# Four small moves in a float32 kernel: Gelu tiles, paired spatial products, late sums of squares, one square on ScalarE

## The reference

```python
# first block, layers 0 and 1
h = rmsnorm(x, g_pre); u, z = split(h @ w_in)            # 2048 -> 2 x 4096
y = pool_mixer(u) if layer 0 else rglru(causal_conv(u))
x = x + rmsnorm((y * silu(z)) @ w_out, g_post)
gate = sigmoid(rmsnorm(x, g_ple_in) @ w_ple_gate)        # 2048 -> 2048
x = x + rmsnorm((p @ w_ple) * gate, g_ple_out)
# second block, layers 2 and 3
proj = rms_norm(x, norm_g) @ w_in
y_a = mla(c_q, c_kv, k_rope) * silu(z_a)                 # attention, 8 heads
y_b = gelu(u_b) * mix(rms_norm(gelu(v_b), v_g)) * silu(z_b)
#     mix: per chunk of 128 tokens and per group of 128 features,
#     tril(w_s) @ v + b_s, 8 groups
y_c = gla(q_c, k_c, v_c, a_r) * silu(z_c)                # gated linear attention, 4 heads
x = x + (sum of sigmoid(gate_b) * (y_b @ w_branch_b)) @ w_out
```

## Time and profile before

| what | us |
|---|---|
| timed runs, median of 3 | 3372.26 (3371.91 to 3381.12) |
| the profiled execution's own time | 3364.99 |
| span of the profiled execution | 3363.2 |
| TensorE matmul busy | 3326.3 (99%) |
| VectorE busy | 2299.5 (68%) |
| ScalarE busy | 1680.0 (50%) |
| GpSimd busy | 947.9 (28%) |

### The profile page before, as it was taken

The page is one execution under the profiler, slowest core; times in us unless marked ns, Lnnn a source line. Parts: engine busy times, 40 slices in busy tenths (PEclk is TensorE's granted clock), DMA queues, the critical chain, the costliest instruction groups (busy, mean ns, idle before and its releaser), DMA issues.

```text
span 3363.2 us, 67501 instructions
## 1 busy us (share of the span) xinstructions
PE 3326.3 (99%) x28712; PEld 3313.3 (99%) x28712; DVE 2299.5 (68%) x3008; ACT 1680.0 (50%) x2122; POOL 947.9 (28%) x901
## 2 busy tenths in 40 slices
PE   8999999999999999999999999999999999999999
PEld 8999999999999999999999999999999999999999
DVE  7876654688888845877867755555568777655554
ACT  5334444555588745655544444444456444444443
POOL 3952320144556500513523200000016222100000
PEclk9999999999999999999999999999999999999999
DMA  6555665556655665555444555555654444555555
GB/s 233 184 188 194 195 221 196 167 178 214 192 179 182 211 212 182 193 167 172 151 155 151 160 195 193 195 195 193 196 173 157 163 145 151 189 194 194 194 190 180
DMA packets 170059, 620.34 MB, mean 184 GB/s; under 512 B 18976, under 2 KB 20640, under 8 KB 169376
## 3 DMA queue, kind: packets, MB, share of 16 engines
q1 hardware_dynamic: 165888, 602.23, 54.2%
q10 hardware_dynamic: 3872, 13.80, 1.1%
HBM read 610.71 MB, written 4.19 MB: 183 GB/s over the span
## 4 chain that ended last, share of the span: by engine, by line
PE 85%; DVE 7%; POOL 4%; ACT 3%; issue 1%; DMA 0%; POOLq 0%; ACTq 0%; SPq 0%; DVEq 0%
PE banks L532 22%; PE banks L524 22%; PE banks L525 22%; PE pm L532 3%; PE pm L525 3%; PE pm L524 3%; DVE w_lo L1240 2%; POOL win L1948 2%; ACT w_hi L857 1%; PE banks L569 1%; PE banks L562 1%; PE banks L564 1%; DVE wide L1262 1%; PE pm L569 1%; PE pm L562 1%
## 5 line engine op out<-in xcount | busy, mean ns | idle before, releaser
L1240 DVE TENSOR_TENSOR w_lo<-raw,w_hi 128x1024 fp32r<-128x1024 f32 x1144 | 1472.6, 1291 | 845.7 <-ACT w_hi L857 831.9
L857 ACT ACTIVATE w_hi<-raw 128x1024 fp32r<-128x1024 f32 x1144 | 1205.6, 1057 | 980.5 <-PE banks L532 720.3
L524 PE MATMUL banks<-xs,w_hi 128*128 128x256 f32 x4520 | 1068.6, 278 | 0.3 <-ACT val L1131 0.3
L525 PE MATMUL banks<-xs,w_hi 128*128 128x256 f32 x4520 | 1068.4, 278 | 0.0
L524 PEld LDWEIGHTS banks<-xs,w_hi 128*128 128x128 f32 x4520 | 854.7, 189 | 0.7 <-ACT val L1131 0.7
L525 PEld LDWEIGHTS banks<-xs,w_hi 128*128 128x128 f32 x4520 | 854.6, 189 | 0.0
L532 PE MATMUL banks<-xs,w_lo 128*128 128x256 f32 x4520 | 626.0, 281 | 1.0 <-DVE w_lo L1240 1.0
L532 PEld LDWEIGHTS banks<-xs,w_lo 128*128 128x128 f32 x4520 | 564.9, 189 | 2.1 <-DVE w_lo L1240 1.4
L1871 POOL CAST merged<-act 128x256 fp32r<-128x256 f32 x32 | 40.3, 1258 | 714.4 <-DVE act L1661 714.4
L524 PE MATMUL pm<-xs,w_hi 128*128 128x256 f32 x952 | 224.7, 278 | 0.0
L525 PE MATMUL pm<-xs,w_hi 128*128 128x256 f32 x952 | 224.3, 277 | 0.0
(11 more groups left out here) (326 smaller groups left out, 5725.4 us busy)
## 6 DMA issues: line engine op xcount, KB each, us to landing
raw<-weights SPq DMA_DIRECT2D x1144, 512.0 KB, 3.4
wide<-x_in ACTq DMA_DIRECT2D x4, 512.0 KB, 8.8
wide<-x_in ACTq DMA_DIRECT2D x1, 2048.0 KB, 12.2
x_scratch<-wide ACTq DMA_DIRECT2D x1, 2048.0 KB, 9.2
wide<-x_scratch ACTq DMA_DIRECT2D x1, 2048.0 KB, 11.3
out_x<-wide SPq DMA_DIRECT2D x3, 512.0 KB, 4.9
w_st<-w_s ACTq DMA_DIRECT2D x2, 512.0 KB, 4.5
b_st<-b_s ACTq DMA_DIRECT2D x2, 512.0 KB, 5.7
```

What stands on the lines that cost most here:

```text
L524: nc.tensor.matmul(bank, w_hi[:, slot, w], x[:, 0:T], start=(k + t == 0), stop=False)
L525: nc.tensor.matmul(bank, w_hi[:, slot, w], x[:, T:2 * T], start=False, stop=False)
L857: nc.scalar.activation(w_hi[:, slot, :], raw[:, slot, :], ACT.Copy).then_inc(hi_done, 1)
L1240: nc.vector.tensor_tensor(w_lo[:, slot, :], raw[:, slot, :], w_hi[:, slot, :].bitcast(F32), ALU.subtract).then_inc(lo_done, 1)
```

## The change

There are four parts.

1. The Gelu of vb's tiles 6 and 7. VectorE runs tile 6 after the reads of uq's first unit and tile 7 after those of its third, each ahead of the side work of that unit. ScalarE makes the tanh of tile 7 in uq's second unit. GpSimd's program is as before: the squares of tiles 6 and 7 at the end of vb, then the side work of uq.
2. The spatial products of two groups go to the two halves of one bank. TensorE waits from g = 4 on and only for every second group, VectorE waits for both groups of a pair at once.
3. `sum_squares` begins with a wait for all six chunks of x. ScalarE's square of the fourth block moves behind the split of unit 9 (it stood ahead of unit 8).
4. At the end of gate ScalarE squares tile 14 (to `val` 1), GpSimd sums tiles 0 to 13 only. TensorE has 6 warm-up products instead of 10 and takes each of the three sources as it comes.

```diff
-            stages[-1].counts = {"t": ND, "q": ND, "p": ND - 1}
+            stages[-1].counts = {"t": ND, "q": ND, "p": ND - 2}
...
@@ TensorE, spatial_gate
-                    if g >= 2:
-                        pe.wait_ge(sgu_read, q - 1)
+                    if g >= 4 and g % 2 == 0:
+                        pe.wait_ge(sgu_read, q - 2)
                     for chunk in range(2):
-                        ins = nc.tensor.matmul(pm[:, g % 2, chunk * P:(chunk + 1) * P],
+                        at = (g % 2) * T + chunk * P
+                        ins = nc.tensor.matmul(pm[:, (g // 2) % 2, at:at + P],
@@ TensorE, end of gate
-                    keep_warm(10)
-                    pe.wait_ge(pool_done, s.end["p"])
-                    pe.wait_ge(sq_last, l + 1)
-                    mean_square(l, "gate", [acc[:, :], val[:, 0, :]])
+                    keep_warm(6)
+                    pe.wait_ge(root_ready, norms[l, "gate"])
+                    for j, (a, made, at) in enumerate(((acc[:, :], pool_done, s.end["p"]),
+                                                       (val[:, 1, :], sq_ahead, l + 1),
+                                                       (val[:, 0, :], sq_last, l + 1))):
+                        pe.wait_ge(made, at)
+                        ins = nc.tensor.matmul(ms_bank[:, 0:T], mean_d[:, :], a, start=(j == 0), stop=(j == 2))
+                    ins.then_inc(ms_ready, 1)
@@ ScalarE, fed_turn
-                squares(f, 3)
                 for u in range(8, 2 * s.units):
                     split(u)
+                    if u == 9:
+                        squares(f, 3)
@@ ScalarE, turn and end of stage
+                        if s.name == "uq" and u == 1:
+                            gelu_tanh(7)
...
                     gate_tanh(ND - 1)
+                    sc.wait_ge(res_ready, s.base["q"] + ND - 1)
+                    nc.scalar.activation(val[:, 1, :], gated[:, ND - 2, :], ACT.Square).then_inc(sq_ahead, 1)
                     scale_gated(ND - 2)
                     scale_gated(ND - 1)
-                if s.name in ("vb", "ub"):
+                if s.name == "ub":
                     gelu_tanh(7)
+                if s.name in ("uq", "ub"):
                     gelus += 1
@@ VectorE, spatial_gate
-                    ve.wait_ge(sgu_mix, c * S_GROUPS + g + 1)
+                    if g % 2 == 0:
+                        ve.wait_ge(sgu_mix, c * S_GROUPS + g + 2)
...
-                        in0=pm[:, g % 2, 0:T].rearrange("p (c t) -> p c t", t=P),
+                        in0=pm[:, (g // 2) % 2, (g % 2) * T:(g % 2 + 1) * T].rearrange("p (c t) -> p c t", t=P),
@@ VectorE, turn and end of stage
+                        if s.name == "uq" and u in (0, 2):
+                            gelu(stages[n - 1], 6 + u // 2)
...
-                    gelu(6)
-                    gelu(7)
+                    if s.name == "ub":
+                        gelu(s, 6)
+                        gelu(s, 7)
@@ GpSimd
             def sum_squares(f):
+                wait(gp, x_updated, f * len(CHUNKS))
...
+                    if s.name == "gate" and m >= ND - 2:
+                        return
```

More of the change, by code:

```diff
@@ L263, in build @@
                                                       sem("root_ready"), sem("rstd_ready"))
-        sq_used, sq_last, sq_summed, scaled = sem("sq_used"), sem("sq_last"), sem("sq_summed"), sem("scaled")
+        sq_used, sq_ahead, sq_last, sq_summed, scaled = sem("sq_used"), sem("sq_ahead"), sem("sq_last"), sem("sq_summed"), sem("scaled")
         lru_root, lru_p, lru_at, lru_m, lru_b, lru_y = (
@@ L1715, in second, with gelu @@
                             nc.vector.tensor_tensor(val[:, 0, :], g_, g_, ALU.mult).then_inc(sq_last, 1)
-                def gelu(m):
+                def gelu(s, m):
                     v, a = val[:, m % 4, :], act[:, m % 4, :]
@@ L1811, in turn @@
                                 if m >= 2:
-                                    gelu(m - 2)
+                                    gelu(s, m - 2)
                             else:
@@ L1975, in post @@
                         gp.wait_ge(pool_done, m + (s.base["p"] + 1))
-                    elif s.name == "gate" and m < ND - 1:
+                    elif s.name == "gate":
                         gp.wait_ge(res_ready, m + (s.base["q"] + 1))
```

## The result

The changed kernel takes 3387.05 us (median of 20 runs, 3377.37 to 3409.04), the kernel before 3372.73 beside it (20 runs, 3362.57 to 3392.71): ratio 1.0041, 95% interval 1.0026 to 1.0057. It is 14.3 us slower, where 0.7 us less was forecast. Its own profiled execution, 3405.93 us, lies near the top of its runs; what can be said of that stands further down. One execution of before beside e1 to e4 took 5571.33 us at a mean granted clock of 0.556, and the ratios of e1 to e4 leave it out.

A forecast was written before the change was run, and what follows sets the result against it. TensorE, busy 3326.3 of 3363.2 us, bounds the kernel through matmul count, waits and half clock. Gelu +11.2, pairs -8.5, squares -2.8 and gate -0.6 sum to -0.7 us: 3371.6 us, range 3358 to 3382.

The forecast's parts named there:

- The first wait in uq goes, L619 is late next: In uq, TensorE's 2.4 us wait for q_buf vanishes, but L619 starts 3.9 us later, its keys queued behind tile 7.
- the upper end: In uq, worst case per layer: L619 5.3 us late, and a clock drop costing 3.4 us.
- The clock in uq, 1.7 a layer: In uq, after TensorE's stand at L619, a half-clock drop costs 1.7 us per layer.
- GpSimd gets in only when VectorE pauses.: In the feeds, VectorE's unbroken instructions delay GpSimd's sums, the last to 783.1 in conv's; TensorE stands 0.9 us there.
- -2.8: Squares summed after x is written: 4.6 us of w_lo delay go, 1.8 us of standing come, net -2.8 us.
- Pairs, -8.5: Spatial products by pairs: stalls give -3.9 us in all, shorter half clock -2.3 us per layer.
- Rival C: At the spatial products, the pairs bring no clock back, all else as forecast: 3376.2 us, chance 0.12.
- Gate, -0.6: At the end of gate, rms starts 0.3 us earlier, twice: -0.6 us.
- B: In uq, GpSimd kept out, two clock drops, +8.7 us twice; pairs -3.9, feeds and gate nothing: 3385.8 us, chance 0.14.

The follow-up runs named there:

- e1: Against the kernel before, only the Gelu of vb's tiles 6 and 7 moved into uq: 3383.97 us, ratio 1.0037.
- e4: Against the kernel before, only the end of gate changed (ScalarE's square, fewer warm-up products): 3368.82 us, ratio 0.9997.
- e5: Kernel before with the Gelu part, and GpSimd making L619's keys ahead of the squares of tiles 6 and 7: 3376.53 us, ratio 0.9996.
- e6: Kernel before with only the sums of squares moved, to wait for the eleventh unit's w_lo instead of x's update: 3367.81 us, ratio 0.9991.
- e3: Against the kernel before, only the spatial products go by pairs: 3364.23 us, ratio 0.9982.
- e9: The whole changed kernel, plus GpSimd making L619's keys before squaring vb's tiles 6 and 7: 3371.82 us, ratio 0.9996 to the kernel before.
- e11: Kernel before with Gelu part, pairs and gate part, keys ahead of the squares, sums of squares unmoved; a repeat run: 3350.79 us, ratio 0.9942.
- e10: All four parts, keys ahead of the squares, sums of squares after the eleventh unit's w_lo; a repeat run: 3351.06 us, ratio 0.9937.

## Why the prediction was wrong

The forecast was 3371.6 us, the result 3387.05, 15.4 more. The base was right (before measured 3372.73); the sum was not. By starts the parts came to +15.2 instead of -0.7: 8.7 us of the difference lie in the squares, where VectorE was held and not GpSimd, 6.4 in the Gelu part, where the sizes were too small, 1.1 in the pairs. By its own steps:

- **The first wait in uq goes, L619 is late next.** Right in place, order and cause; e1 and e5 show it from both sides. The size failed. "GpSimd then takes 0.7 for the square, 0.7 for the sum and 1.7 for the keys": the square took 2.20 us instead of 0.7, for it ended only behind a w_lo that VectorE began inside it (1666.89, 1.22 us); and the 9.5 us of VectorE to the end of tile 7's Gelu were 10.6 (w_lo 1.41 and 1.76 instead of 1.15, Gelu 0.86 instead of 0.4). 2.9 + 1.5 + 1.1 = 5.5 of the measured 5.8, where I took 3.9 and put the upper end at 5.3. My upper end had both delays in, but for the square only 0.7 of the 1.5, and I took a value below it; both came.
- **The clock in uq, 1.7 a layer.** By starts each layer lost 7.7 and 9.9 us; less the 5.8 that is 1.9 and 4.1. In e1, with the same stall, 2.1 and 2.3. Layer 2 is near my 1.7, layer 3 above even the 3.4 of my upper end; on average 3.0, so the term was too small. Together the Gelu part cost +17.6 (+12.5 timed alone) for +11.2.
- **"GpSimd gets in only when VectorE pauses."** This step failed, and it made -2.8 out of +5.9. I took it from one sum of 5.73 us that lay under three w_lo, and made it a rule for every sum. In conv's feed the sum at 762.18 got in between two w_lo that follow each other without a pause, and then sums and VectorE's instructions took turns: the fourth sum ended at 772.8, 774.3 in before's time (the feed's first w_lo stands 1.5 us earlier), not at 783.1. So ms_bank, for which I feared, was served early, and w_lo, which I had as safe, was late. The Trainium skill (SBUF — State Buffer, Who interferes with whom) says that issue order decides who blocks. Here the trace agrees in conv's feed, where the sum of 762.18 holds the w_lo of 763.10, and differs in gate's, where three w_lo begun after the sum of 671.19 pass it. The 5.73 us of the earlier trace rows was no exception: in each of before's four feeds the third sum took 4.6 to 5.8 us. Both outcomes occur, and the loss comes where the third sum gets in. The skill's rule alone didn't lead to the cost: I had worked it out for one w_lo held, and there were four sums in a row. In uq I had gone the other way: there I took the square at its bare 0.7, and it was held out. What the move really did: before, each sum followed its own square, one by one with pauses of 4.9 us between them; after, the data lay ready and in conv's feed the four came as one block of 10.6 us, in front of the w_lo that TensorE needed. e6, in which only their place differs, has the 4.6 us.
- **Pairs, -8.5.** The stall went, the banks were right; the stretch at half behind the second pair fell from 6.8 to 3.4 us in both layers. -7.4 by starts, -10.6 and -6.1 in e3 by starts and timed (-5.8 and -9.0 without the 1.6 us of before's own): right within what can be told. In layer 3 of the change two further stretches behind it lost 1.6 us each, so that layer had 10.2 us at half as before. Rival C is out by all profiled executions together: from the spatial products on, layers 2 and 3 together had 6.8 to 23.9 us at half in the seven with the pairs, 27.3 to 34.1 in the seven without.
- **Gate, -0.6.** -0.4 a layer, by rms 4.22 to 3.85 us, in every kernel that had the edit. Right; by time alone it can't be told.
- **The rivals.** B gave 3385.8 and its point of decision, L619 after 1659, was passed: 1660.2. In uq that is nearly what happened. That the total fits as well is partly luck, for B had no loss in the feeds and less gain from the pairs. I gave it 0.14 because GpSimd's short steps of before weren't slowed behind the reciprocal; but with the Gelu moved, the square no longer stood there, it stood beside a w_lo.

## What to carry to other kernels

When a step moves to another place, price it and all that is queued behind it by its new neighbours, not by its duration at the old one: GpSimd's 0.7 us square cost 2.20 beside a w_lo, and VectorE's low parts 6.98 instead of 1.67 beside the sums. A wait that gathers several jobs of GpSimd can turn spaced holds of VectorE into one block (conv and gqk; not gate), so place it where the engine that feeds TensorE has a lead (e6), and let what TensorE needs next go first in GpSimd's program (e5 and e9: one line ends two waits of 9.4 us). And where an order is only inherited, look for the job that stands ahead of the urgent one before moving anything later.

## What the runs showed of the hardware that I had not expected

TensorE's products of the same shape run at 113.3 or 117.8 ns from start to start for up to 500 us at a stretch, with the clock granted in full. It makes 20 to 50 us of an execution (20 in e11, 25 in before, 37 in e10, 50 in the changed kernel's), more than this whole change. That it makes one kernel's runs spread over 30 us isn't shown: only profiled executions show it, and while the changed kernel's (50) and e4's (42) stand 19 us above their medians, e9's (39) is the fastest of its runs. The switches come, with one exception in fourteen executions, at a distance of 0.2 us or more or beside products of another shape; what decides which of the two follows isn't settled here. The granted clock doesn't show it: only the count of products in a stretch does. And an instruction of GpSimd that meets VectorE isn't simply slow or simply fast: in the changed kernel sums of the same shape took 2.39 to 6.85 us, and VectorE pays where they are short.
